# Five norms of 256 tokens: 1/rms put on at the output of the next GEMM instead of at its input

## The reference

```python
def rms_norm(x, gain):
    xf = x.astype(jnp.float32)
    y = xf * lax.rsqrt(jnp.mean(xf * xf, axis=-1, keepdims=True) + RMS_EPS)
    return (y * gain).astype(x.dtype)

def modulate(x, gain, shift, scale):
    return rms_norm(x, gain) * (1 + scale) + shift

def swiglu(h, w_in, w_out):
    a, b = jnp.split(h @ w_in, 2, axis=-1)
    return (jax.nn.silu(a) * b) @ w_out
...
    x = x + 0.5 * swiglu_2(rms_norm_2(x, g_ffn1[layer]), w_ffn1_gu[layer], w_ffn1_down[layer])
    h = rms_norm_2(x, g_mix[layer])
    proj = h @ w_in[layer]
```

## Time and profile before

| | us |
|---|---|
| median of 3 runs | 2650.06 |
| lowest, highest | 2649.21, 2651.81 |
| span of the profiled execution | 2648.0 |
| TensorE busy in it | 2542.6 |
| VectorE, ScalarE, POOL busy | 1354.5, 1089.6, 244.2 |

### The profile page before, as it was taken

The page is one execution under the profiler, slowest core; times in us unless marked ns, Lnnn a source line. Parts: engine busy times, 40 slices in busy tenths (PEclk is TensorE's granted clock), DMA queues, the critical chain, the costliest instruction groups (busy, mean ns, idle before and its releaser), DMA issues.

```text
span 2648.0 us, 45172 instructions
## 1 busy us (share of the span) xinstructions
PE 2542.6 (96%) x17855; PEld 1668.0 (63%) x17855; DVE 1354.5 (51%) x1911; ACT 1089.6 (41%) x1610; POOL 244.2 (9%) x235
## 2 busy tenths in 40 slices
PE   6999999999999999999999899999999999989999
PEld 4444444456544444444444568878888888777887
DVE  7556434453465553365532544365556554555664
ACT  6444323243354442244433311355445544444553
POOL 1143000004000000100003100021010010010001
PEclk8999999999999999999999999999999999999999
DMA  9896632320156653366553333248675755333574
GB/s 301 191 211 191 184 91 64 96 80 1 30 178 190 187 161 107 110 183 190 158 143 92 96 103 90 64 129 238 200 208 171 215 164 155 99 109 108 173 213 127
DMA packets 657854, 383.74 MB, mean 145 GB/s; under 512 B 10908, under 2 KB 654337, under 8 KB 657609
## 3 DMA queue, kind: packets, MB, share of 16 engines
q1 hardware_dynamic: 653432, 369.27, 47.7%
q0 software_dynamic: 3728, 10.98, 2.7%
q10 hardware_dynamic: 576, 1.83, 0.2%
HBM read 380.96 MB, written 1.08 MB: 144 GB/s over the span
## 4 chain that ended last, share of the span: by engine, by line
PE 89%; DVE 7%; ACT 2%; issue 1%; SPq 1%; POOL 0%; DMA 0%; ACTq 0%; DVEq 0%; POOLq 0%
PE PS L636 24%; PE PS L637 23%; PE PS L638 23%; PE PS L750 2%; PE PS L655 1%; PE PS L654 1%; PE PS L653 1%; DVE arena L1568 1%; DVE WL L1394 1%; PE PS L776 1%; PE PS L923 1%; PE PS L613 1%; DVE XL L1574 1%; ACT WH L1003 1%; PE PS L596 1%; PE PS L597 1%
## 5 line engine op out<-in xcount | busy, mean ns | idle before, releaser
L636 PE MATMUL PS<-XH,WH 128*128 128x256 f16 (+1 forms) x2912 | 947.9, 326 | 32.5 <-DVE XL L1574 18.5
L637 PE MATMUL PS<-XL,WH 128*128 128x256 f16 (+1 forms) x2912 | 947.5, 325 | 0.0
L638 PE MATMUL PS<-XH,WL 128*128 128x256 f16 (+1 forms) x2912 | 946.8, 325 | 0.0
L1394 DVE SCALAR_TENSOR_TENSOR WL<-W,WH 128x1024 f16<-128x1024 f32 (+1 forms) x520 | 664.9, 1317 | 285.2 <-ACT WH L1003 285.1
L1003 ACT ACTIVATE WH<-W 128x1024 f16<-128x1024 f32 (+1 forms) x520 | 551.0, 1106 | 603.6 <-PE PS L638 501.7
L636 PEld LDWEIGHTS PS<-XH,WH 128*128 128x128 f16 x2912 | 287.4, 99 | 221.6 <-issue 33.1
L638 PEld LDWEIGHTS PS<-XH,WL 128*128 128x128 f16 x2912 | 288.1, 99 | 181.4 <-issue 4.7
L637 PEld LDWEIGHTS PS<-XL,WH 128*128 128x128 f16 x2912 | 287.8, 99 | 171.4 <-issue 4.0
L636 PE MATMUL PS<-arena,WH 128*128 128x256 f16 (+1 forms) x1184 | 378.9, 320 | 1.9 <-DVE WL L1394 1.9
L637 PE MATMUL PS<-arena,WH 128*128 128x256 f16 (+1 forms) x1184 | 378.9, 320 | 0.0
L638 PE MATMUL PS<-arena,WL 128*128 128x256 f16 (+1 forms) x1184 | 378.9, 320 | 0.0
(11 more groups left out here) (239 smaller groups left out, 2345.2 us busy)
## 6 DMA issues: line engine op xcount, KB each, us to landing
arena<-in_w_mod SPq DMA_DIRECT2D x72, 1024.0 KB, 8.7
W<-in_ffn_a_in SPq DMA_DIRECT2D x88, 512.0 KB, 5.1
W<-in_ffn_b_in SPq DMA_DIRECT2D x88, 512.0 KB, 4.7
W<-in_w_ffn_gu SPq DMA_DIRECT2D x88, 512.0 KB, 4.3
W<-in_ret_in SPq DMA_DIRECT2D x48, 512.0 KB, 4.3
W<-in_ffn_a_out SPq DMA_DIRECT2D x32, 704.0 KB, 5.5
W<-in_ffn_b_out SPq DMA_DIRECT2D x32, 704.0 KB, 5.9
W<-in_w_ffn_down SPq DMA_DIRECT2D x32, 704.0 KB, 5.6
```

The lines of the kernel that those rows point to most:

```text
L636: mm(dst, wh, xh, start=(kp == 0 and c == 0), stop=False, skip_group_check=True)
L637: mm(dst, wh, xl, start=False, stop=False, skip_group_check=True)
L638: return mm(dst, wl, xh, start=False, stop=(kp == g["parts"] - 1 and c == kc - 1), skip_group_check=True)
L1394: stt(WL[:, k, t, 0:g["kc"], :], W32[:, k, t, 0:g["kc"], :], W_SCALE, WH[:, k, t, 0:g["kc"], :], ALU.mult, ALU.subtract).then_inc(lo_ready, 1)
```

## The change

For norms 5, 6, 7, 9 and 10 the copy XH of X times gain is made by ScalarE right behind each square, and XL by VectorE (`late_rest`), during the residual GEMM; norms 9 and 10 use the other half of XH and XL, since mix_out and cross_out read the first. The next GEMM's first block starts from these; the sums stand behind its chunk 1 and the spread behind its chunk 4. ScalarE copies the spread 1/rms from PSUM to RR. It is put on at the output: `store` becomes two operations with RR (mix_v, whose tokens lie on partitions, uses `rstd_col`, RR turned by two TensorE transposes), and in an FFN VectorE first scales gate and up half from PSUM to SBUF (`late_drain`), ScalarE's silu reads the scaled gate, VectorE multiplies (`late_product`), and hidden and rest follow. `shift` of norm 5 becomes a 257th column of the input, whose output column is added as a per-partition bias. The tables H0 and HH0 count h_ready without these norms. Left out below: declarations of tiles and semaphores, the fields `late` and `N` of a GEMM, and the renamed counts.

```diff
@@ -376,6 +380,19 @@
+LATE = {5: 0, 6: 0, 7: 0, 9: SEQ, 10: SEQ}
+
+def late_rhs(at, N):
+    return lambda kp, c, T, kc: (XH[:, c, at:at + N], XL[:, c, at:at + N])
+
+for n, names in ((5, ("ffn_1b_in",)), (6, ("ffn_2a_in",)), (7, ("mix_q", "mix_k", "mix_v")), (9, ("cross_q",)), (10, ("ffn_2b_in",))):
+    for name in names:
+        g = next(x for x in GEMMS if x["name"] == name)
+        g["late"] = n
+        g["N"] = SEQ + 1 if n == 5 else SEQ
+        g["rhs"] = late_rhs(LATE[n], g["N"])
+LATE_FFNS = ["ffn_1b_in", "ffn_2a_in", "ffn_2b_in"]
+
 MOD_BLOCKS = N_MOD * DC
...
@@ -659,13 +680,17 @@
                     for t in range(2):
-                        ins = three(PS[:, 2 * pair + t, 0:T], t, k, kp, c)
+                        ins = three(PS[:, 2 * pair + t, 0:g["N"]], t, k, kp, c)
+                    if g["late"] is not None and c == 1:
+                        pe_sums(g["norm"], (0, DC - 1))
+                    if g["late"] is not None and c == 4:
+                        pe_spread(g["norm"])
             else:
...
-                        dst = PS[:, pair, SEQ * t:SEQ * t + SEQ] if g["packed"] else PS[:, 2 * pair + t, 0:T]
+                        dst = PS[:, pair, SEQ * t:SEQ * t + SEQ] if g["packed"] else PS[:, 2 * pair + t, 0:g["N"]]
                         ins = three(dst, t, k, kp, c)
...
@@ -688,8 +713,9 @@
                     between[b]()
-            pe_sums(g["then"], (0, DC - 1))
-            pe_spread(g["then"])
+            if g["then"] not in LATE:
+                pe_sums(g["then"], (0, DC - 1))
+                pe_spread(g["then"])
             return
...
@@ -968,11 +994,15 @@
         ins.then_inc(mem_turned, 1)
+    pe.wait_ge(rstd_held, LATE_AT[7] + 1)
+    for t in range(2):
+        ins = turn(PS[:, BANK_N + 1, P * t:P * t + P], RR[:, P * t:P * t + P], eye)
+    ins.then_inc(rstd_turned, 1)
     pe_gemm(gi["mix_k"])
...
     pe.wait_ge(units_drained, drained(gi["mix_k"]))
-    pe.wait_ge(h_ready, H0[MEM_NORM + 1])
+    pe.wait_ge(h_ready, HH0[MEM_NORM + 1])
     pe.wait_ge(rel_back, 32)
...
@@ -1047,11 +1077,19 @@
         def silu(i, k):
+            if g["late"] is not None:
+                bias = shift_out[:, k, 0:1] if g["N"] > T else 0.0
+                act.wait_ge(units_drained, u0 + k + 1 + 2 * i)
+                act.activation(ffn_s[:, k, 0:T], ffn_s[:, k, T:2 * T], ACT.Silu, bias=bias).then_inc(silu_done, 1)
+                return
             act.wait_ge(block_used, g["w0"] + k + 1 + 2 * i)
...
         def hidden(i, k):
-            act.wait_ge(units_drained, u0 + k + 1 + 2 * i)
+            if g["late"] is not None:
+                act.wait_ge(hidden_ready, FC * LATE_FFNS.index(g["name"]) + k + 1 + 2 * i)
+            else:
+                act.wait_ge(units_drained, u0 + k + 1 + 2 * i)
             copy(GH[:, bass.ds(2 * i + k, 1), 0:T], ffn_g[:, k:k + 1, 0:T]).then_inc(gh_done, 1)
...
@@ -1093,6 +1131,8 @@
             act.activation(N["sq"][:, c, 0:N["T"]], N["src"][:, c, 0:N["T"]], ACT.Square).then_inc(sq_ready, 1)
+            if n in LATE:
+                copy(XH[:, c, LATE[n]:LATE[n] + SEQ], X[:, c, 0:SEQ], N["a"](c, 0)).then_inc(xh_ready, 1)
...
@@ -1110,7 +1150,15 @@
         squares(n, range(2 * done, DC))
-        act_norm(n, after)
+        if n not in LATE:
+            act_norm(n, after)
+            return
+        split(after, 0, 1, tiles=(0,))
+        act_root(n)
+        split(after, 0, 1, tiles=(1,))
+        act.activation(warm[:, 0:1], mats[:, 1, 0:1], ACT.Silu)
+        act.wait_ge(rstd_ready, n + 1)
+        copy(RR[:, :], PS[:, BANK_N + 1, 0:SEQ]).then_inc(rstd_held, 1)
...
@@ -1458,6 +1506,18 @@
+        def late_drain(i, k):
+            dve.wait_ge(block_used, w0 + k + 1 + 2 * i)
+            stt(ffn_g[:, k, T:2 * T], PS[:, 2 * k + 1, 0:T], 1.0 / W_SCALE, RR[:, :], ALU.mult, ALU.mult)
+            if g["N"] > T:
+                ts(shift_out[:, k, :], PS[:, 2 * k:2 * k + 2, T:T + 1].rearrange("p a b -> p (a b)"), 1.0 / W_SCALE, None, ALU.mult)
+            stt(ffn_s[:, k, T:2 * T], PS[:, 2 * k, 0:T], 1.0 / W_SCALE, RR[:, :], ALU.mult, ALU.mult).then_inc(units_drained, 1)
+
+        def late_product(i, k):
+            dve.wait_ge(silu_done, FC * g["ffn"] + k + 1 + 2 * i)
+            shift = shift_out[:, k, 1:2] if g["N"] > T else 0.0
+            stt(ffn_g[:, k, 0:T], ffn_g[:, k, T:2 * T], shift, ffn_s[:, k, 0:T], ALU.add, ALU.mult).then_inc(hidden_ready, 1)
+
         def rest(i, k):
...
@@ -1465,6 +1525,16 @@
             dve.wait_ge(block_used, w0 + k + 1 + 2 * i)
+            if g["late"] is not None:
+                for t in range(2):
+                    if g["tok"]:
+                        ins = ts(g["dest"][:, t, bass.ds(512 * i + 256 * k, 256)], PS[:, 2 * k, 256 * t:256 * t + 256],
+                                 1.0 / W_SCALE, rstd_col[:, t:t + 1], ALU.mult, ALU.mult)
+                    else:
+                        ins = stt(g["dest"][:, bass.ds(4 * i + 2 * k + t, 1), 0:T], PS[:, 2 * k + t:2 * k + t + 1, 0:T], g["scale"] / W_SCALE,
+                                  RR[:, :].rearrange("p (a n) -> p a n", a=1), ALU.mult, ALU.mult)
+                ins.then_inc(units_drained, 1)
+                return
             if g["tok"]:
...
@@ -1485,7 +1555,23 @@
             return
-        if g["kind"] == "ffn":
+        if g["late"] is not None:
+            dve.wait_ge(rstd_held, LATE_AT[g["late"]] + 1)
+        if g["kind"] == "ffn" and g["late"] is not None:
+            with dve.Fori(1, n) as i:
+                for k in range(2):
+                    late_drain(i - 1, k)
+                    split(g, i, k)
+                    late_product(i - 1, k)
+                    rest(i - 1, k)
+            for k in range(2):
+                late_drain(n - 1, k)
+                if k == 0:
+                    split(after, 0, 0)
+                late_product(n - 1, k)
+                rest(n - 1, k)
+            split(after, 0, 1)
+        elif g["kind"] == "ffn":
             for lo, hi, mods in ((1, g["mods"], True), (max(g["mods"], 1), n, False)):
...
@@ -1515,8 +1601,13 @@
+    def late_rest(n, c):
+        N, at = NORMS[n], LATE[n]
+        dve.wait_ge(xh_ready, H0[n] + c + 1)
+        stt(XL[:, c, at:at + SEQ], X[:, c, 0:SEQ], N["a"](c, 0), XH[:, c, at:at + SEQ], ALU.mult, ALU.subtract).then_inc(xl_ready, 1)
+
     def dve_resid(g, after, between={}):
-        T, nb = g["T"], g["blocks"]
+        T, nb, late = g["T"], g["blocks"], g["then"] in LATE
...
@@ -1537,13 +1628,27 @@
                 between[b]()
+            if late and b < nb:
+                for c in range(halves, 2 * u):
+                    late_rest(g["then"], c)
+                halves = 2 * u
         if after is not None:
             split(after, 0, 0)
+        if late:
+            for c in range(halves, 6):
+                late_rest(g["then"], c)
         dve.wait_ge(early_used, g["r"] + 1)
         add(3, (0,)).then_inc(early_added, 1)
+        if late:
+            late_rest(g["then"], 6)
         dve.wait_ge(block_used, g["w0"] + nb)
         add(3, (1,)).then_inc(units_drained, 1)
-        dve_norm(g["then"], after)
+        if late:
+            late_rest(g["then"], 7)
+            dve_inverse(g["then"])
+            split(after, 0, 1)
+        else:
+            dve_norm(g["then"], after)
...
@@ -1774,6 +1879,10 @@
     gated(RET_HEADS - 1)
+    at = (N_MOD + 6) * DC
+    shift, shift_hi, shift_lo = modT[:, at:at + DC, 0:1], XH[:, :, SEQ:SEQ + 1], XL[:, :, SEQ:SEQ + 1]
+    link(dve.tensor_copy(shift_hi, shift))
+    tt(shift_lo, shift, shift_hi, ALU.subtract)
     run("ret_out")
...
@@ -1781,6 +1890,8 @@
     run("mix_k")
+    dve.wait_ge(rstd_turned, 1)
+    link(dve.tensor_copy(rstd_col[:, :], PS[:, BANK_N + 1, 0:SEQ].rearrange("p (t n) -> p t n", t=2)[:, :, 0]))
     dve_inverse(MEM_NORM)
```

More of the change, by code:

```diff
@@ L162, in program @@
         warm = sb("warm", [P, 2])
+        RR = sb("RR", [P, SEQ])
+        shift_out = sb("shift_out", [P, 2, 2])
+        rstd_col = sb("rstd_col", [P, 2])
         relvec = sb("relvec", [N_HEADS_2, BOTH])
@@ L277, in program @@
         fin_turned, fin_copied, stored = sem("fin_turned"), sem("fin_copied"), sem("stored")
+        rstd_held, hidden_ready, rstd_turned = sem("rstd_held"), sem("hidden_ready"), sem("rstd_turned")
         ROWS = [("b_mod", 0, 0, 72), ("norm_gain", None, 72, 48), ("c", None, 120, 8),
@@ L309, in gemm @@
             g = dict(name=name, kind=kind, w=w, kc=kc, blocks=blocks, T=T, cols=cols, rhs=rhs, parts=parts, tok=tok,
-                     dest=dest, scale=scale, gate=gate, ffn=ffn, units=blocks // parts, need=list(need), need_2=need_2, norm=norm, mods=0, m0=0, packed=name == "ret_g")
+                     dest=dest, scale=scale, gate=gate, ffn=ffn, units=blocks // parts, need=list(need), need_2=need_2, norm=norm, mods=0, m0=0, packed=name == "ret_g", late=None, N=T)
             last = GEMMS[-1] if GEMMS else None
@@ L481, in program @@
             H0.append(H0[-1] + DC * (N["T"] // SEQ))
```

(10 more changed lines are left out.)

## The result

| | us |
|---|---|
| median after, 4 runs (lowest, highest) | 2684.55 (2681.36, 2688.99) |
| median before, 4 runs (lowest, highest) | 2649.77 (2649.21, 2651.81) |
| ratio, 95% interval | 1.0117 [1.0101, 1.0134] |
| profiled execution of after, its span | 2688.99, 2687.0 |

Slower by 34.8 us between the medians, where 21 were forecast; 2684.55 lies inside the range 2654 to 2688, near its upper end. The medians' quotient is 1.0131, inside the interval; the ratio of 1.0117 stands for 31 us (27 to 36). The four executions of before in this table are at the fast end of its scatter: the medians of its larger sets, run beside the experiments, are 2653.87 and 2653.52. TensorE got 6.8 us busier and the span 39.0 us longer.

What follows compares the result with a forecast made beforehand. TensorE was taken to bound the kernel, busy 96% of the span. Losses of 17.1, twice 11.1, 1.8 and 0.4 us less 20.5 at four boundaries gave +21.0: span 2669.0, median 2671 us, range 2654 to 2688.

Steps and rivals of the forecast that it cites:

- Part 1: Five stretches from a residual GEMM's end through the next first block: 42.0 us for 68.5, a gain of 26.5.
- Part 2: FFN blocks' drain: VectorE's scaling makes blocks 5.84 us for 5.24, losing 11.1 us each in ffn_2a_in and ffn_2b_in.
- The ring: FFN input blocks: VectorE and ScalarE wait for each other in turn without overlap, 5.69 us by durations, 5.84 in all.
- register work: Loop's addresses and wait values behind two waits in an FFN block: 0.15 us taken in all, branch costed at nothing.
- the slack of 0.9: First block of an FFN output GEMM: VectorE's split may lag 0.9 us before TensorE is delayed.
- Part 3: ffn_1b_in: blocks of 6.10 us with the shift, held weight loads eat the boundary's 6.0 us gain; loss 17.1 us.
- Part 4: Store GEMMs: second scaling operation costs nothing, at most 5 us uncovered; RR's two turns cost about 0.4 us.
- (a): Rival: FFN blocks are not bound by VectorE and ScalarE, boundary gains stand; 2624 to 2630 us, chance 0.07.
- (b): Rival: FFN turns take only 5.5 to 5.69 us and block 3's weights come early; 2650 to 2658, chance 0.09.
- (c): Rival: sums wait for POOL and spread for the root inside first blocks, 2 us at each of five; 2681, chance 0.07.
- (d): Rival: TensorE's short pauses in every FFN block halve its clock at times; 2740 us, chance 0.02.
- The rule against the row: VectorE successions in FFN blocks: trace's 0.08 us overlap preferred to the skill's no-overlap rule, which would give near 2694.

Runs made afterwards that it cites:

- x4: The change for norms 7 and 9 alone (mix_q, cross_q), the three FFNs as before: 2643.91 us, ratio 0.9961 to the kernel before.
- x8: The changed kernel with ScalarE's and VectorE's FFN input loops written out for the three late FFNs: 2670.41 us, ratio 1.0074 to before.
- x5: The changed kernel with POOL's loads of rel_bias and mem moved to ffn_1b_out, in four pieces of 1 MB: 2681.6 us, ratio 1.0112 to before.
- x1: The changed kernel with ScalarE's split of the next weights ahead of silu in the FFN input GEMMs: 2640.85 us, ratio 0.9954 to before.
- x6: The changed kernel with ScalarE's split ahead of silu and POOL's loads moved to ffn_1b_out in four pieces: 2634.21 us, ratio 0.9928 to before.
- x2: The changed kernel with the gate half scaled first and silu waiting for that alone: 2664.91 us, ratio 1.0054 to before.
- x3: The changed kernel with one more VectorE addition of 256 columns behind the rest in each block: 2705.89 us, ratio 1.0192 to before.
- x7: The changed kernel with ScalarE's split ahead of silu and POOL's loads in eight 0.5 MB pieces over ffn_1b_in: 2636.33 us, ratio 0.9935 to before.

## Why the prediction was right, and where it was off

**Part 1, right.** 41.9 us against 42.0 forecast. The sums waited 0.19 us for POOL behind ret_out, the narrow place that the prediction named, and 0.14 each behind mix_out and cross_out; nothing waited for the root. The copies and rests put into the residual blocks cost nothing there: in x4 ffn_2a_out and mix_out took 57.64 and 20.97 as before.

**Part 2, the mechanism right, one term too small.** The ring was forecast as 5.69 by durations and 0.15 for register work, bounds 0 to 0.32. The durations held: x8 shows 5.695 a block. The register work and branch take 0.32 (6.02 less 5.695), the upper end of the bounds; I took their middle, and costed the branch at nothing. So the blocks of 6.02 lie outside the 5.8 to 5.9 that the forecast named as its sign, while ring, queues and waits are those that it named. (The splits of 1408 columns take 1.38 and 1.62 us; by the ratio that the prediction names they would be 1.44 and 1.68, not its 1.41 and 1.63. It moves the slack of 0.9 by under 0.1.) The forecast's own rule with 6.02 gives 20 x 0.78 - 0.9 = 14.7 us for an FFN; measured, less the boundary's gain, 14.8 (10.0 + 4.8) and 14.8 (9.4 + 5.4). The output GEMMs' 1.8 came as forecast.

**Part 3, right, and late by the same term.** The ring of ffn_1b_in is 6.235 (forecast 6.10; the shift's operation and the pointers cost 0.22, forecast 0.26), and block 2 was scaled 28.6 us behind ret_out's end for 27.6 forecast: 0.55 for weights and product, 0.46 of register work between product and scaling. 18 x 0.135 + 1.0 = 3.4 on top of 17.1 gives 20.5; the measured difference is 20.6. That the held DMAs eat this boundary's gain was right too: x5 takes the pause away and ffn_1b_in gets 7.3 us shorter.

**Part 4.** The store GEMMs cost nothing that a record shows; what is left between ffn_2a_out's end and mix_k, where RR's turns stand, is 0.7 us, forecast 0.4 (35.35 less 4.7 of the boundary is 30.6, measured 31.3). The 257th column costs 0.04 us a block once TensorE bounds again (5.28 for 5.24 in x1 and x6), 0.9 for the GEMM, forecast 0.4.

**The sum.** Forecast +21.0; with the register work at its measured size (18 x 0.135 + 40 x 0.18 = 9.6) and ffn_1b's 1.0 it is +31.6; the terms measured +32.1. The step that failed is a choice within bounds, "I take 0.15 in all, the middle": a small term that is multiplied by 58 rings decides the size. The ratio's 31 us (27 to 36) agree with that; the 34.8 between the medians are 2.7 more, which the low scatter of before's four executions can account for.

**The rivals.** (a), the ring doesn't bind: wrong for the changed kernel, but x6 is what it describes. Its sum was a gain of 26.1 us; x6's span is 18.1 under before's although 6.6 are lost elsewhere (2.3 ahead of the change, 2.2 in ffn_1b_out, 2.1 in mix_out), so 24.7 without these, and 0.9 go to the 257th column. (b) needed a ring under 5.69 and weights that come early; the ring of the durations is 5.695 and with the loop 6.02. (c), waits inside the first block: 0.19, 0.14 and 0.14 us for POOL in three of the five, none for the root. (d), a halved clock from short pauses: the granted clock was 1.00 in all three ring-bound stages (1850 to 1951, 2030 to 2142 and 2505 to 2615 of after, and the like ones of x2 and x3), with a pause of 0.4 us (5.61 less 5.24) to 1.3 us (6.57 less 5.28) in each block. The second failure mode of the clock gate in the Trainium skill (TensorE: Matmul & The Clock Gate, A second HAM failure mode) doesn't show here.

**The rule against the row.** The row decided rightly. VectorE's succession of alike operations kept its overlap of 0.08 us in all of these kernels, 2.36 for two splits of 1.22. By the rule of the Trainium skill (VectorE: DVE Perf Modes, The DRAIN you can't avoid) as I read it the ring would be 6.1 without register work; x8 shows 5.695. A later section of the same page (Two Vector instructions with no wait between them) says that only a held instruction waits for the finish of all earlier ones; the overlap in these rows agrees with these operations not being held.

## What to carry to other kernels

Before an operation is put between a matmul and what reads it, follow the queues of both engines once around a block: if work of the next block stands behind the wait for it, the sum start to start is a floor for the block, however idle each engine is. Opening the ring was a change of order alone here and cost nothing: the next block's split ahead of silu turned 1.2% slower into 0.5% faster. In a ring count what a loop works out between two links, and multiply every uncertain tenth by the number of blocks before choosing a middle.

## What the runs showed of the hardware that was not expected

Register work and branch of a loop: 0.32 us a block where it stands in a ring through two engines (6.02 against 5.695 in x8), while the same loops in the kernel before left each block at 5.24.

Queued DMAs: in 1806 to 1832 of after three loads of POOL (4 MB together) and SyncE's weight loads share the engines. DMA issues in that window, with KB each and median us to landing:

```profile
W<-in_ffn_b_in SPq DMA_DIRECT2D x5, 512.0 KB, 13.7
arena<-rel_scratch POOLq DMA_DIRECT2D x1, 2048.0 KB, 16.4
arena<-rel_scratch POOLq DMA_DIRECT2D x1, 1024.0 KB, 9.8
arena<-in_mem POOLq DMA_DIRECT2D x1, 1024.0 KB, 18.3
```

The page has a median of 4.7 us for the same weight load over the whole span. In x7's ffn_1b_in the same 4 MB pass with a DMA share of 0.86 and no wait, so it is not the total that hurts. Whether it is the size of a piece, its distance to the next or the stage that it falls in was not taken apart: x7 changed all three against x5 and x6.

Where a half-clock stretch falls: at the end of the block attention TensorE pauses for 3.7 us (before, up to 2354.18) or 3.3 us (after, up to 2386.69), and around that pause the granted clock is 0.50. Before, then after, then a stretch near the start of the same attention in after, which before doesn't have:

```profile
2350.80:2357.60 6.80, 3.42 (x16) 2.78 (x16) 4.75 (x16) 4.05 (x14) 0.00 (x0) 0.50 0.51 151
...
2382.30:2396.00 13.70, 9.31 (x41) 6.84 (x42) 7.17 (x19) 5.91 (x15) 0.00 (x0) 0.50 0.27 77
...
2286.70:2293.50 6.80, 6.80 (x25) 4.14 (x23) 1.73 (x4) 1.02 (x4) 0.00 (x0) 0.50 0.84 233
```

In after the long stretch reaches 4.4 us into mix_out, which takes 23.09 for 20.97. So it does in x3, x5, x6 and x7 (23.0 to 23.2), while x1, x2, x4 and x8 have 20.97 as before has. The other stretch, in which TensorE is busy throughout, is where the 2.8 us between mix_k and mix_out are: after and x3 have it with 6.8 us at half clock and take 159.55 from start to start, x5 and x7 have one of 3.4 us and take 159.0, before, x1, x2, x4, x6 and x8 have none there and take 156.6 to 157.4. The pause ahead of it, 2.3 us for 1.9 in before, is as long in the kernels that have no such stretch. The work ahead of the change scatters too: ret_out ends anywhere from 1802.3 to 1814.6 us in these profiles, nearly all of it from the very first FFN's input GEMM, the same instructions in all (some 254 us in x8, 263 in x3, which has 10.2 us at half clock from 184.0 where x8 has none). What picks the one or the other stays open; a span read from one profile is uncertain by 2 to 5 us by these, once by 10, which is why the sums above go by the length of stages.
